# A state space mixer whose real and imaginary state products are merged: states and output matrices stacked on the partitions, 64-row products replaced by 128-row products in two column halves

## The reference

```python
def s5_mixer(u, ...):                       # u: (1, 512, 1024) = 64 groups of 16 channels
    ab = exp((lam_re + 1j*lam_im) * dt)     # per group 64 complex states, a diagonal recurrence
    bu = einsum('gpc,blgc->blgp', bb, u)    # bb complex
    x[t] = ab * x[t-1] + bu[t]              # complex, over the 512 positions
    y = einsum('gcp,blgp->blgc', c_re, x_re) - einsum('gcp,blgp->blgc', c_im, x_im) + d * u
    z = gelu(y); return z * sigmoid(z @ w_glu)
```

## Time and profile before

| | |
|---|---|
| time, median of 3 runs | 2295.32 us (2295.04 to 2296.09) |
| span of the profiled execution | 2293.4 us |
| what lies around the span (median less span) | 1.9 us |
| TensorE busy | 2255.4 us, 98% |
| VectorE, ScalarE, GpSimd busy | 44%, 36%, 18% |
| mean granted TensorE clock | 0.998 of full |
| the eight `pe_y` pieces | first at 294.1 us, last at 662.0 us of the span |

### The profile page before, as it was taken

One profiled execution on the slowest core, in us unless ns is written; L12 is line 12 of the kernel. 1 busy time (PEld: TensorE's weight loads), 2 busy tenths in 40 slices (PEclk: granted clock), 3 DMA queues, 4 the chain that ended last, 5 costly groups with the idle time before them and its releaser, 6 DMA issues.

```text
span 2293.4 us, 30844 instructions
## 1 busy us (share of the span) xinstructions
PE 2255.4 (98%) x11901; PEld 1831.9 (80%) x11901; DVE 998.4 (44%) x1865; ACT 823.4 (36%) x1457; POOL 402.1 (18%) x691
## 2 busy tenths in 40 slices
PE   7999999999999999999999999999999999999998
PEld 7888887787788878888788778888887866788886
DVE  4632455444522256643353442442122356666534
ACT  6533333333332434432342223322232444555323
POOL 1626113222221011100010001100000254221100
PEclk9999999999999999999999999999999999999999
DMA  7645444434445346563344446444443665454632
GB/s 281 205 136 138 132 112 126 125 115 136 117 116 189 102 159 197 176 222 101 117 145 122 133 144 226 129 133 151 153 123 97 210 201 168 144 194 135 227 102 92
DMA packets 166923, 345.65 MB, mean 151 GB/s; under 512 B 21535, under 2 KB 32111, under 8 KB 164355
## 3 DMA queue, kind: packets, MB, share of 16 engines
q1 hardware_dynamic: 106832, 188.51, 27.3%
q0 software_dynamic: 31248, 98.44, 13.5%
q10 hardware_dynamic: 28707, 56.84, 6.8%
HBM read 279.89 MB, written 63.83 MB: 150 GB/s over the span
## 4 chain that ended last, share of the span: by engine, by line
PE 96%; issue 1%; DVE 1%; ACT 1%; DMA 1%; DVEq 0%; POOL 0%; SPq 0%; ACTq 0%; POOLq 0%
PE PS L241 79%; PE PS L1699 3%; PE PS L2365 2%; PE PS L1688 2%; PE PS L291 1%; PE PS L1122 1%; PE PS L2262 1%; PE PS L558 1%; PE PS L1870 1%; PE PS L2225 1%; PE PS L1448 1%; PE PS L2014 1%; PE PS L2258 1%; PE PS L1895 1%; PE PS L1118 1%
## 5 line engine op out<-in xcount | busy, mean ns | idle before, releaser
L241 PE MATMUL PS<-A,wsp 128*128 128x512 f32 (+2 forms) x5184 | 1160.4, 384 | 1.7 <-ACT stage L344 1.2
L241 PEld LDWEIGHTS PS<-A,wsp 128*128 128x128 f32 (+1 forms) x5184 | 942.3, 188 | 198.6 <-issue 8.8
L210 DVE TENSOR_TENSOR wsp<-wraw,wsp 128x1024 fp32r<-128x1024 f32 (+1 forms) x358 | 432.8, 1210 | 991.7 <-ACT wsp L203 990.6
L241 PE MATMUL PS<-wsp,A 128*128 128x512 f32 x2928 | 752.0, 401 | 3.6 <-DVE stage L1770 1.7
L203 ACT ACTIVATE wsp<-wraw 128x1024 fp32r<-128x1024 f32 (+1 forms) x358 | 372.1, 1042 | 911.2 <-PE PS L241 879.2
L241 PEld LDWEIGHTS PS<-wsp,A 128*128 128x128 f32 x2928 | 532.1, 189 | 103.9 <-issue 9.1
L344 ACT ACTIVATE stage<-PS 128x512 f32<-128x512 f32 (+1 forms) x150 | 87.1, 587 | 141.3 <-PE PS L241 136.7
L1735 ACT ACTIVATE S<-PS 128x256 f32<-128x256 f32 (+3 forms) x160 | 62.9, 393 | 121.9 <-PE PS L1688 121.0
L1743 ACT ACTIVATE S<-PS,stats 128x256 f32<-128x256 f32 (+3 forms) x160 | 74.8, 467 | 74.8 <-DVE stats L1780 63.6
L1699 PEld LDWEIGHTS PS<-S 128*128 128x128 f32 x640 | 93.0, 191 | 10.3 <-issue 1.1
L1699 PE MATMUL PS<-S 128*128 128x128 f32 x640 | 94.3, 274 | 0.6 <-issue 0.6
(11 more groups left out here) (342 smaller groups left out, 1729.4 us busy)
## 6 DMA issues: line engine op xcount, KB each, us to landing
wraw<-in_even_w_in_dram SPq DMA_DIRECT2D x112, 512.0 KB, 3.7
wraw<-in_odd_w_in_dram SPq DMA_DIRECT2D x88, 512.0 KB, 3.6
wraw<-in_w_out_dram SPq DMA_DIRECT2D x80, 512.0 KB, 3.7
wraw<-in_mem_w_kv_dram SPq DMA_DIRECT2D x32, 512.0 KB, 4.5
yO<-stage ACTq DMA_DIRECT2D x12, 1024.0 KB
yE<-stage ACTq DMA_DIRECT2D x10, 1024.0 KB
S<-yO POOLq DMA_DIRECT2D x36, 256.0 KB, 3.5
hA<-stage ACTq DMA_DIRECT2D x8, 1024.0 KB
```

The lines of the kernel that those rows point to most:

```text
L210: nc.vector.tensor_tensor(wsp[:, q, 1, :, 0:j["cols"]], wraw[:, q, :, 0:j["cols"]], wsp[:, q, 0, :, 0:j["cols"]].bitcast(F32), ALU.subtrac ...
L241: mm = nc.tensor.matmul(dst, lhs, rhs, start=(s == 0 and kk == 0 and i == 0), stop=(s == j["spc"] - 1 and kk == 1 and i == 2))
```

## The change

`stS` and `WO` are laid out anew: the partition index is now (i, state), real part on partitions 0 to 63 and imaginary part on 64 to 127, and the group of a pair, e, is on the free axis. One product over 128 rows then sums the real and the imaginary part of one group, and the two groups take the two column halves, as the products of line 1118 already do. For this `dve_wo` no longer uses `dve_product`: it makes the four partial products into four buffers (RS, tA, tB and a new one, tC, 2 KB a partition) and combines them in four operations on 64 partitions each, some of which read one half of the partitions and write the other. `dve_r` writes the states in four operations on 64 partitions instead of two on 128. The semaphore counts follow (8 and 11 a round).

```diff
@@ layouts
-        WO = S[:, 3776:4800].rearrange("p (i j s c) -> p i j s c", i=2, j=4, s=8)
+        WO = S[:, 3776:4800].rearrange("p (e j s c) -> p e j s c", e=2, j=4, s=8)
+        tC = sb("tC", [P, 512])
-        stS = high(520).rearrange("p (i j n) -> p i j n", i=2, j=4)
+        stS = high(520).rearrange("p (e j n) -> p e j n", e=2, j=4)
@@ dve_wo
-                dve.wait_ge(r_step, 9 * m)
-            dve_product(dve, wo_step, m, WO, cc[:, 0, 4 * m:4 * m + 4, :], cc[:, 1, 4 * m:4 * m + 4, :], 0, -1)
+                dve.wait_ge(r_step, 11 * m)
...
+            nc.vector.tensor_tensor(rr, cr, by[0], ALU.mult).then_inc(wo_step, 1)
+            nc.vector.tensor_tensor(ii, ci, by[1], ALU.mult).then_inc(wo_step, 1)
+            nc.vector.tensor_tensor(ri, cr, by[1], ALU.mult).then_inc(wo_step, 1)
+            nc.vector.tensor_tensor(ir, ci, by[0], ALU.mult).then_inc(wo_step, 1)
+            for i in range(2):
+                dve.wait_ge(wo_step, n + 2 + 2 * i)
+                for e in range(2):
+                    q = slice(64 * e, 64 * e + 64)
+                    dst = WO[64 * i:64 * i + 64, e]
+                    if i == 0:
+                        nc.vector.tensor_tensor(dst, rr[q], ii[q], ALU.add).then_inc(wo_step, 1)
+                    else:
+                        nc.vector.tensor_tensor(dst, ir[q], ri[q], ALU.subtract).then_inc(wo_step, 1)
@@ dve_r
-            nc.vector.tensor_tensor(stS[:, 0, :, 1:65], A2[:, 0], B2[:, 1], ALU.subtract).then_inc(r_step, 1)
-            nc.vector.tensor_tensor(stS[:, 1, :, 1:65], A2[:, 1], B2[:, 0], ALU.add).then_inc(r_step, 1)
+            for e in range(2):
+                q = slice(64 * e, 64 * e + 64)
+                nc.vector.tensor_tensor(stS[0:64, e, :, 1:65], A2[q, 0], B2[q, 1], ALU.subtract).then_inc(r_step, 1)
+                nc.vector.tensor_tensor(stS[64:128, e, :, 1:65], A2[q, 1], B2[q, 0], ALU.add).then_inc(r_step, 1)
@@ pe_y
                 for e in range(2):
                     nc.tensor.matmul(dst[e], US[:, 2 * j_ + e, :], MT[:, 2 * j_ + e, :], start=True, stop=False)
-                for i in range(2):
-                    for e in range(2):
-                        q = slice(e * 64, e * 64 + 64)
-                        mm = nc.tensor.matmul(dst[e], stS[q, i, j_, 0:64], WO[q, i, j_].rearrange("p s c -> p (s c)"), start=False, stop=(i == 1))
+                for e in range(2):
+                    mm = nc.tensor.matmul(dst[e], stS[:, e, j_, 0:64], WO[:, e, j_].rearrange("p s c -> p (s c)"), start=False, stop=True)
```

More of the change, by code:

```diff
@@ L959, in act_tab @@
             if m:
-                act.wait_ge(r_step, 9 * m)
+                act.wait_ge(r_step, 11 * m)
             nc.scalar.activation(sinS, fS, ACT.Sin, scale=TWO_PI).then_inc(tab_ok, 1)
@@ L964, in act_tab, with dve_product @@
             nc.scalar.activation(cosS, cosS, ACT.Sin, scale=-TWO_PI, bias=half_pi).then_inc(tab_ok, 1)
-        def dve_product(dve, step, n, out, cr, ci, k0, sign):
+        def dve_product(dve, step, n, out, cr, ci, k0):
             by = [pw[:, i, k0:k0 + 8, 4 * n:4 * n + 4].rearrange("p k j -> p j k").unsqueeze(3).broadcast_to([P, 4, 8, 16]) for i in range(2)]
@@ L975, in dve_product @@
             dve.wait_ge(step, 6 * n + 2)
-            nc.vector.tensor_tensor(out[:, 0], out[:, 0], tmp[0], ALU.subtract if sign > 0 else ALU.add).then_inc(step, 1)
+            nc.vector.tensor_tensor(out[:, 0], out[:, 0], tmp[0], ALU.subtract).then_inc(step, 1)
             dve.wait_ge(step, 6 * n + 4)
[L978 to L981, removed]
+            nc.vector.tensor_tensor(out[:, 1], out[:, 1], tmp[1], ALU.add).then_inc(step, 1)
         def dve_bp(dve, m):
@@ L989, in dve_bp @@
                 dve.wait_ge(set_pe, 3 * m)
-                dve.wait_ge(wo_step, 6 * m)
-            dve_product(dve, bp_step, m, BP, bc[:, 0, 4 * m:4 * m + 4, :], bc[:, 1, 4 * m:4 * m + 4, :], 1, 1)
+                dve.wait_ge(wo_step, 8 * m)
+            dve_product(dve, bp_step, m, BP, bc[:, 0, 4 * m:4 * m + 4, :], bc[:, 1, 4 * m:4 * m + 4, :], 1)
         def dve_wo(dve, m):
@@ L996, in dve_wo @@
                 dve.wait_ge(y_pe, m)
-                dve.wait_ge(r_step, 9 * m)
-            dve_product(dve, wo_step, m, WO, cc[:, 0, 4 * m:4 * m + 4, :], cc[:, 1, 4 * m:4 * m + 4, :], 0, -1)
+                dve.wait_ge(r_step, 11 * m)
+            n = 8 * m
+            by = [pw[:, i, 0:8, 4 * m:4 * m + 4].rearrange("p k j -> p j k").unsqueeze(3).broadcast_to([P, 4, 8, 16]) for i in range(2)]
+            cr, ci = [cc[:, i, 4 * m:4 * m + 4, :].unsqueeze(2).broadcast_to([P, 4, 8, 16]) for i in range(2)]
+            rr, ii, ri, ir = [v.rearrange("p (j s c) -> p j s c", j=4, s=8) for v in (RS, tA, tC[:, :], tB)]
+            nc.vector.tensor_tensor(rr, cr, by[0], ALU.mult).then_inc(wo_step, 1)
[11 more added lines that the diff above has]
+                        nc.vector.tensor_tensor(dst, ir[q], ri[q], ALU.subtract).then_inc(wo_step, 1)
         def dve_k(dve, m):
@@ L1009, in dve_r @@
         def dve_r(dve, m):
-            n = 9 * m
+            n = 11 * m
             flat = lambda v: v.rearrange("p (i j n) -> p i j n", i=2, j=4)
@@ L1017, in dve_r @@
             dve.wait_ge(bp_step, 6 * min(m + 2, 8))
-            dve.wait_ge(wo_step, 6 * (m + 1))
+            dve.wait_ge(wo_step, 8 * (m + 1))
             nc.vector.tensor_tensor(A2, BU, both(cosS), ALU.mult).then_inc(r_step, 1)
@@ L1111, in pe_y @@
             pe.wait_ge(k_ev, 2 * (m + 1))
-            pe.wait_ge(wo_step, 6 * (m + 1))
+            pe.wait_ge(wo_step, 8 * (m + 1))
             pe.wait_ge(m_in, 128 * (m + 1))
-            pe.wait_ge(r_step, 9 * (m + 1))
+            pe.wait_ge(r_step, 11 * (m + 1))
             for j_ in range(4):
@@ L2499, in _ @@
             pool.wait_ge(y_pe, 8)
-            pool.wait_ge(r_step, 72)
+            pool.wait_ge(r_step, 88)
             pool.wait_ge(stored, 16 * (E1["stored0"] + 2))
```

## The result

The changed kernel takes 2281.14 us (median of 4, 2279.03 to 2284.39) where the kernel before takes 2295.24 (median of 4, 2295.04 to 2296.09): ratio 0.9935, interval [0.9923, 0.9947]. The forecast was 2279.9 us. Two later comparisons with the same kernel gave 2279.84 (5 runs, beside 2295.58) and 2279.59 (5 runs, beside 2295.89), ratios 0.9934 [0.992, 0.9947] and 0.9931 [0.9917, 0.9944]. So the gain is 14.1, 15.7 and 16.3 us for a forecast of 15.4. The span of the profiled execution is 2277.4 us, forecast 2278.0.

What follows compares the result with a forecast made beforehand. TensorE was taken to bound the kernel. Eight rounds of 1.93 us less in `pe_y` (passes 7.0, changes 8.4) gave -15.4 us, VectorE's work hidden: 2295.3 - 15.4 = 2279.9 us, range 2277.0 to 2288.5.

Steps and rivals of the forecast that it cites:

- What bounds the kernel: In the mixer's stretch, 286 to 814 us, TensorE is always busy, so time taken off it comes off the end.
- The pass and the change of block: In `pe_y`, a pass costs 0.109 us, a change between 128-row and 64-row blocks 0.15; gain 1.93 us a round.
- the changes stay: In `pe_y`, if all changes between blocks remain, only eight passes a round are gained: 7.0 us instead of 15.4.
- rival 1: Loss between `pe_y` blocks hangs on fresh sources or new accumulation, not shape: gain 7.0 us, time 2288.3; chance 0.07.
- The quadrants: In `pe_y`, the trace was held to contradict the skill's four independent 64x64 tiles, by which only 8.4 us would be gained.
- rival 2: Each `pe_y` pass must pay a weight load of 0.134 us: +1.8 us in all, time 2297.1; chance 0.02.
- VectorE: Added work of +1.2 us in `dve_wo` and +0.7 in `dve_r` a round, about 15 us in all, stays hidden.
- Rival 3: Slow `dve_r` state operations across partition halves make `pe_y` wait; at 2 us each, time 2306; chance 0.03.

## Why the prediction was right

**What bounds the kernel** held: 15.4 us taken off TensorE (8 x 1.92) came off the span. From the start of the first piece to the end of the last it is 356.2 us where it was 371.7, 15.5 less. The span fell by 16.0. The other 0.5 is 0.9 before the first piece (it starts at 293.3 us instead of 294.1, in other executions of the changed kernel at 293.6 and 294.0), less 0.4 behind the last one; both differ by as much from one execution to the next.

**The pass and the change of block** are shown apart: both alone (24 passes without changes 2.77 us, 16 passes with eight changes 2.94 us, forecast 2.77 and 2.94), and both together 1.90 for a forecast of 1.89. The bound of 7.0 us for "the changes stay" was not needed, and rival 1 is refuted by the kernel with its state products twice. The prediction had no row for 128-row products from different sources side by side; that no change is left between them was argued from line 1098 and came true.

**The quadrants** were argued wrongly, though nothing of the sum hung on it: the four state products of a pair lay in two quadrants, so they could not have run all at once there. Counting passes needs the tile of each record as well as the number of records: equal tiles take turns, different ones don't.

**Weight loads** (rival 2) stayed hidden: 0.22 us for a block of four records with all 128 rows in use, each with a load of 0.137 us. The rule of the Trainium skill, "TensorE: Matmul & The Clock Gate", Part 3, section The mechanism, that loads overlap running matmuls only where the row group differs, does not hold for this shape here. The prediction left out that the same section of the Trainium skill also lets a load go ahead into a background weight buffer; with that the trace agrees.

**VectorE** was mis-sized and hidden, as forecast. `dve_wo` grew by 1.55 us for a forecast of 1.2, `dve_r` by 1.13 (from 0.68 between the start of the state operations and the next split to 1.81) for 0.7, together 21 us for a forecast of 15. The value taken for the distance was that of operations on 128 partitions, 0.35; those that alternate between partition halves stand 0.45 apart, as operations of this size do that wait for their predecessor (0.46 at lines 948 to 952 of the kernel before). That it is the change of half that holds them was not tested. The margin ahead of `pe_y` is 2.91 us.

**Rival 3** did not come, since an operation across partition halves takes 0.42 us. As a mechanism it is real, and its threshold of 3.9 us over the kernel before (3.0 in round 0) was right: at 1.13 + 2.15 = 3.28 only round 0 waits, 0.3 us, and beyond it TensorE waits one for one. Its price left out the clock.

## What to carry to other kernels

Where TensorE is the chain, count small float32 products in passes (records side by side in different tiles count once) and in changes of array shape; more than half of this gain (8.4 of 15.4 us) was changes. Lay data out so that neighbouring products have one shape, even at the price of more and smaller operations on an engine with slack. Measure that slack at the one consumer that waits, and treat it as a cliff: past it, a wait can cost clock as well (1.6 us on top of 2.24 here, in five rounds of eight).

## What was not expected of the hardware

- A change of shape costs the same in either direction between 128*64 and 64*64, 0.15 us (0.37 us from block to block either way, for two passes of 0.109). Between 64*128 and 128*32 the first start behind it comes as soon as that of a full-size projection (0.64 us).
- Transposes that fill 64 columns (line 1139) are entered without a loss: they start 0.23 us after the last projection (497.67 to 497.90), a projection's own distance, where `pe_y` starts 0.32 after it.
- Waits of TensorE of 2.2 us (3.2 in round 0), one every 53 to 55 us, were followed in five rounds of eight by a stretch at 1.2 GHz. This is one execution, that of the kernel with seven additions; without these waits the same stretch of the changed kernel is at 1.00.
